# A quarter of the second-table rows of the expert layer moved from TensorE to a sum kept by VectorE

## What is computed

```python
act = gelu(einsum('thkd,td->thk', u_tab[expert], x))       
out = einsum('thk,thkd->td', gate * act, v_tab[expert])    
x = layer_norm(ALPHA * x + out, ln2_g, ln2_b)
```

## Time and profile before

| | |
|---|---|
| median of three runs | 4074.74 us (4070.53 to 4085.25) |
| the profiled execution, own time | 4068.89 us |
| its span | 4067.1 us |
| mean granted TensorE clock | 0.94 |
| TensorE busy | 3526.3 us, 87% |
| VectorE busy | 2538.4 us, 62% |
| ScalarE busy | 1025.4 us, 25% |
| POOL busy | 2533.5 us, 62% |
| moved by DMA | 1270.02 MB, mean 312 GB/s |

### The profile page before, as it was taken

One profiled execution on the slowest core, in us unless ns is written; L12 is line 12 of the kernel. 1 busy time (PEld: TensorE's weight loads), 2 busy tenths in 40 slices (PEclk: granted clock), 3 DMA queues, 4 the chain that ended last, 5 costly groups with the idle time before them and its releaser, 6 DMA issues. The chain is left out here.

```text
span 4067.1 us, 42088 instructions
## 1 busy us (share of the span) xinstructions
PE 3526.3 (87%) x13480; PEld 2019.6 (50%) x13480; DVE 2538.4 (62%) x6604; ACT 1025.4 (25%) x2150; POOL 2533.5 (62%) x2420
## 2 busy tenths in 40 slices
PE   8787698999999799798999799999999877787878
PEld 6576364555555365344566256545555434222434
DVE  2535986766357985667557985567636798645442
ACT  2231132332122223222322222233312222211211
POOL 0212447877675655877765655687766666777773
PEclk9778799999999899999999999999999989999999
DMA  5015888888999898888999988888999989999996
GB/s 183 21 64 183 287 328 320 302 322 328 350 356 372 324 354 333 320 312 294 349 340 386 364 289 318 290 320 308 339 336 343 379 301 358 385 374 362 370 398 228
DMA packets 331050, 1270.02 MB, mean 312 GB/s; under 512 B 38336, under 2 KB 39616, under 8 KB 313808
## 3 DMA queue, kind: packets, MB, share of 16 engines
q0 software_dynamic: 299520, 1090.65, 73.0%
q1 hardware_dynamic: 31312, 176.67, 11.4%
HBM read 1259.74 MB, written 7.44 MB: 312 GB/s over the span
## 5 line engine op out<-in xcount | busy, mean ns | idle before, releaser
L819 PE MATMUL Y<-GV,DIAG 128*128 128x512 f32 x4096 | 1993.3, 624 | 315.4 <-DMA GV<-in_vtab,IDX 249.9
L1759 DVE SCALAR_TENSOR_TENSOR GU<-GU,X 128x1024 f32<-128x1024 f32 x1024 | 1241.4, 1230 | 511.2 <-DMA GU<-in_utab,IDX 508.9
L1038 POOL DMA_INDIRECT GU<-in_utab,IDX x1024 | 1152.5, 1125 | 641.4 <-DVE GU L1759 295.8
L1038 POOL DMA_INDIRECT GV<-in_vtab,IDX x1024 | 1146.1, 1119 | 597.8 <-PE Y L819 374.2
L819 PEld LDWEIGHTS Y<-GV,DIAG 128*128 128x128 f32 x4096 | 767.2, 197 | 1285.1 <-issue 985.9
L514 PE MATMUL A<-XT,WR 128*128 128x264 f32 (+1 forms) x2496 | 579.8, 388 | 18.1 <-ACT R L1252 10.5
L1285 ACT ACTIVATE DIAG<-C,WGT 128x128 f32<-128x128 f32 x1024 | 371.5, 392 | 749.1 <-PE Y L819 625.8
L514 PEld LDWEIGHTS A<-XT,WR 128*128 128x128 f32 x2496 | 481.3, 193 | 146.2 <-issue 74.9
L974 POOL TENSOR_TENSOR R<-R 128x256 f32<-128x256 f32 (+3 forms) x256 | 130.1, 541 | 164.6 <-DVE R L1437 88.9
L567 PE MATMUL SCP<-R,C 128*32 128x64 f32 (+3 forms) x512 | 104.6, 361 | 109.9 <-DVE R L1469 109.6
L733 PE MATMUL D<-WR,R 96*128 96x256 f32 (+3 forms) x800 | 189.9, 395 | 11.5 <-POOL R L992 11.5
(11 more groups left out here) (216 smaller groups left out, 2897.3 us busy)
## 6 DMA issues: line engine op xcount, KB each, us to landing
WR<-in_wstream SPq DMA_DIRECT2D x96, 1024.0 KB, 7.8
WR<-in_wstream SPq DMA_DIRECT2D x36, 1280.0 KB, 9.1
GU<-in_utab,IDX POOLq DMA_INDIRECT x1024, 6.5
GV<-in_vtab,IDX POOLq DMA_INDIRECT x1024, 6.5
R<-in_lnp SPq DMA_DIRECT2D x14, 512.0 KB, 7.1
SS<-in_st_in SPq DMA_DIRECT2D x12, 384.0 KB, 4.8
out_st_s<-SS SPq DMA_DIRECT2D x12, 384.0 KB, 6.2
WR<-in_wstream SPq DMA_DIRECT2D x16, 256.0 KB, 6.5
```

Of the source, the lines that this page charges most:

```text
L819: last = nc.tensor.matmul(Y[0:rows, c], scaled, GV[:, v % RV, c], start=(j == 0), stop=(j == end - 1))
L1038: pool.indirect_dma_start(ring[:, i % places, :], None, table, bass.IndirectOffsetOnAxis(ap=idx, axis=0)).then_inc(fetched[i % places], 16)
L1759: nc.vector.scalar_tensor_tensor(out=u, in0=u, scalar=1.0, in1=X[:, tile_of(g), :], op0=ALU.mult, op1=ALU.mult, accum_out=SCORE[:, g % 2, ...
```

## The change

Rows of a block are divided between two engines. `by_vector` names the entries for VectorE: in blocks 0 to 5 slots 6, 10, ..., 126; in the last 24 entries of the kernel every odd slot below 127. For such an entry there is no diagonal and no matmul; VectorE multiplies the row by the tokens' weights and adds it to `YS`, a new tile in SBUF, one tick later than TensorE had it, ahead of the dot. ScalarE starts `YS` as ALPHA times X, one tick after the block's slot 0, and at the block's end VectorE adds `YS` and `Y` into X. The places of `GV` that VectorE empties are refilled on its signal `v_added`, by a fetch that POOL issues one tick later than before and ahead of that tick's first-table fetch. The 4 KB of `YS` come from `SG` and `SCS`, which now lie over `S`.

```diff
+TAIL = NROW - LAG
+def by_vector(v):
+    kind, _, j = ROWS[v]
+    if kind == "s" or not 4 <= j < SLOTS - 1:
+        return False
+    return j % 4 == 2 if v < STEP_AT[3] else v >= TAIL and j % 2 == 1
+VEC = [by_vector(v) for v in range(NROW)]
+VEC_NO = [sum(VEC[:v + 1]) for v in range(NROW)]
+PE_NO = [v + 1 - VEC_NO[v] for v in range(NROW)]
+DIAGONALS = [v for v in range(NROW) if ROWS[v][0] == "b" and not VEC[v]]
...
+        YS = sb("YS", 128, D)
...
-        SG = sb("SG", 128, 2, 256)
+        SG = view(12400, 2, 256)
+        SCS = view(12912, 2, 2 * NKEY)
...
             def accumulate(v):
                 kind, g, j = ROWS[v]
+                if VEC[v]:
+                    return
...
-                    pe.wait_ge(sems["diag_ready"], v + 1 - sum(r[0] == "s" for r in ROWS[:v]))
-                    scaled, rows, end = DIAG[:, v % NDIAG, :], 128, SLOTS
+                    pe.wait_ge(sems["diag_ready"], DIAG_NO[v] + 1)
+                    scaled, rows, end = DIAG[:, DIAG_NO[v] % NDIAG, :], 128, SLOTS
...
+            def late(i):
+                return i >= RV and VEC[i - RV]
             def fetch_v(i):
-                if i >= RV:
-                    pool.wait_ge(sems["v_used"], i - RV + 1)
+                if i >= RV and VEC[i - RV]:
+                    pool.wait_ge(sems["v_added"], VEC_NO[i - RV])
+                elif i >= RV:
+                    pool.wait_ge(sems["v_used"], PE_NO[i - RV])
                 fetch(GV, vtab, v_fetched, RV, i)
...
+                if 0 <= t - 1 + RV - LAG < NROW and late(t - 1 + RV - LAG):
+                    fetch_v(t - 1 + RV - LAG)
                 if 0 <= t + RU < NROW:
                     fetch_u(t + RU)
-                if 0 <= t + RV - LAG < NROW:
+                if 0 <= t + RV - LAG < NROW and not late(t + RV - LAG):
                     fetch_v(t + RV - LAG)
...
+            def begin_sum(t):
+                if t < LAG + 1 or t - LAG - 1 >= NROW:
+                    return
+                v = t - LAG - 1
+                kind, g, j = ROWS[v]
+                if kind == "b" and j == 0 and g in SHARED:
+                    if v:
+                        act.wait_ge(sems["y_read"], groups_before(v))
+                    nc.scalar.activation(YS[:, :], X[:, tile_of(g), :], ACT.Copy, scale=ALPHA) \
+                        .then_inc(sems["sum_begun"], 1)
...
+            def add_row(v):
+                _, g, j = ROWS[v]
+                dve.wait_ge(sems["sum_begun"], SHARED.index(g) + 1)
+                dve.wait_ge(v_fetched[v % RV], 16 * (v // RV + 1))
+                dve.drain()
+                nc.vector.scalar_tensor_tensor(out=YS[:, :], in0=GV[:, v % RV, :], scalar=WGT[:, g % 2, j:j + 1],
+                                               in1=YS[:, :], op0=ALU.mult, op1=ALU.add).then_inc(sems["v_added"], 1)
...
-                dve.wait_ge(sems["v_used"], v + 1)
+                dve.wait_ge(sems["v_used"], PE_NO[v])
+                if kind == "b" and g in SHARED:
+                    dve.drain()
+                    nc.vector.tensor_tensor(x, YS[:, :], Y[:, :], ALU.add).then_inc(sems["y_read"], 1)
+                    return
...
             for t in range(NTICK):
+                if t > LAG and VEC[t - LAG - 1]:
+                    add_row(t - LAG - 1)
                 if t < NROW:
                     dot(t)
```

More of the change, by code:

```diff
@@ L80, with groups_before @@
 NTICK = NROW + LAG
+TAIL = NROW - LAG
[8 more added lines that the diff above has]
+DIAGONALS = [v for v in range(NROW) if ROWS[v][0] == "b" and not VEC[v]]
+DIAG_NO = {v: k for k, v in enumerate(DIAGONALS)}
+SHARED = sorted({ROWS[v][1] for v in range(NROW) if VEC[v]})
+def groups_before(v):
+    return len({r[:2] for r in ROWS[:v]})
 def tile_of(g):
@@ L281 @@
 rms_ready on_scaled on_ready mv_ready rstd_ready x1_ready x2_ready sg_used lb_ready small_init
-u_used v_used idx_ready top_read gate_ready gelu_ready w_ready diag_ready y_read
+u_used v_used v_added sum_begun idx_ready top_read gate_ready gelu_ready w_ready diag_ready y_read
 sample_found sample_gate sample_known sample_idx sample_gelu sample_w""".split()
@@ L367, in build @@
         WGT = sb("WGT", 128, 2, SLOTS)
-        SCS = sb("SCS", 128, 2, 2 * NKEY)
         EFS = sb("EFS", 128, 2, TOPK)
@@ L804, in accumulate @@
                 kind, g, j = ROWS[v]
[L805 to L808, removed]
+                if VEC[v]:
+                    return
+                if j == 0 and v:
+                    pe.wait_ge(sems["y_read"], groups_before(v))
                 if kind == "b":
-                    pe.wait_ge(sems["diag_ready"], v + 1 - sum(r[0] == "s" for r in ROWS[:v]))
-                    scaled, rows, end = DIAG[:, v % NDIAG, :], 128, SLOTS
+                    pe.wait_ge(sems["diag_ready"], DIAG_NO[v] + 1)
+                    scaled, rows, end = DIAG[:, DIAG_NO[v] % NDIAG, :], 128, SLOTS
                 else:
@@ L1278, in diagonal @@
                 kind, g, j = ROWS[v]
-                if kind == "s":
+                if v not in DIAG_NO:
                     return
@@ L1282, in diagonal @@
                     act.wait_ge(sems["w_ready"], PH * g + j // TOPK + 1)
-                if v >= NDIAG:
-                    act.wait_ge(sems["v_used"], v - NDIAG + 1)
-                nc.scalar.activation(DIAG[:, v % NDIAG, :], ident, ACT.Copy, scale=WGT[:, g % 2, j:j + 1]) \
+                k = DIAG_NO[v]
+                if k >= NDIAG:
+                    act.wait_ge(sems["v_used"], PE_NO[DIAGONALS[k - NDIAG]])
+                nc.scalar.activation(DIAG[:, k % NDIAG, :], ident, ACT.Copy, scale=WGT[:, g % 2, j:j + 1]) \
                     .then_inc(sems["diag_ready"], 1)
+            def begin_sum(t):
[8 more added lines that the diff above has]
+                        .then_inc(sems["sum_begun"], 1)
             def exps(t):
@@ L1328, in _ @@
                     diagonal(t + AHEAD - LAG)
+                begin_sum(t)
                 work.run(t)
```

## The result

The changed kernel takes 4055.2 us in the median, the kernel before, measured beside it, 4073.4. The ratio is 0.9937 with a 95% interval of 0.9919 to 0.9955: faster by 0.6%. The medians lie 18 us apart, the ratio is worth 26 us, and the two profiled executions, 4068.89 and 4052.73 us, lie 16 us apart; forecast were 63, to 4006 us. One of the six executions took 4140.8 us at a granted clock of 0.844; it counts in the median and not in the ratio. The span of the profiled one is 4050.9 us.

What follows compares the result with a forecast made beforehand. No one engine bounds every stage; POOL's in-order fetch queue paces ticks, its waits on TensorE limiting the gain. Closings 27, middles 35, openings 0, block ends -8, tail 9: 63 us off 4068.9, so 4006 us, range 3905 to 4090.

Steps and rivals of the forecast that it cites:

- Closings: Closing stages: 48 rows relieve TensorE of 83 us, but DMA has little room; gain 27 us (0 to 35).
- Middles: the failed step: Middle stages: two thirds of POOL's 90 us waits on TensorE gained, 25 us charged for VectorE; net gain 35 us.
- Openings: the second mis-sized term: Opening stages: half of relief and add cost shows, plus 40 and minus 31, stretched fetches 9; net 0.
- The clock, a term put at nothing: TensorE's granted clock: at about 80% busy it need not fall, so no term was given.
- Tail and block ends: Last 24 rows split between both engines, gain 9 us; VectorE's add of row 126 at six block ends, minus 8 us.
- VectorE holds POOL off: Rival: each of 138 adds in openings and middles costs its full 1.3 us; 51 us slower, 4120 us; chance 0.12.
- the 0.38 us that I charged for each add: Openings and middles: fetches stretched by VectorE's adds, 2 times 0.19 us per pass, half of it let show.
- Nothing comes through: Rival: middles even because POOL's queue is the bound, closings give 16 us, tail and block ends cancel; 4052 us, chance 0.15.
- the signs named in advance: Closings: TensorE under 90%, DMA share 0.97 or more; POOL waits some 150/at most 320 us; openings unchanged; mean fetch under 1.2 us.

Runs made afterwards that it cites:

- e1: Changed kernel without VectorE's 197 adds; TensorE stays relieved of those rows, which are left out of the output: 3982.5 us, 0.9761 of the kernel before.
- e13: Kernel before with 91 rows taken from TensorE in the middles only, still fetched but added by nobody: 4044.4 us, ratio 0.9925.
- e7: Kernel before with three rows of four (270) left out in the middles only, without an add: 4009.6 us, ratio 0.9838.
- e2: TensorE adds all rows as in the kernel before, and VectorE makes the 197 adds too, into an unread sum: 4125.0 us, ratio 1.0123.
- e5: Changed kernel with VectorE taking its rows only in the openings, none in middles, closings or tail: 4105.2 us, 1.0068 of the kernel before.
- e8: e1 with four matmuls of zeros on TensorE ahead of 36 waits for the score products: 3971.6 us, 0.9744 of the kernel before.
- e9: e6 with four matmuls of zeros on TensorE ahead of 36 waits for the score products: 4011.9 us, 0.9840 of the kernel before.
- e14: e13 with those 91 rows not fetched either: 3993.0 us, 0.9799 of the kernel before.
- e15: e1 with a POOL memset of 512 columns in each of the 384 ticks of the middles: 4070.8 us, 0.9994 of the kernel before.
- e6: Changed kernel with VectorE taking its rows in middles, closings and tail, none in the openings: 4019.5 us, 0.9859 of the kernel before.

## Why the prediction was wrong

The direction and the mechanism of the closings were right; the size was off by a factor of more than two, because two terms of the sum were too large. By stage the forecast was 27 + 35 + 0 - 8 + 9 = 63 us; the profiled execution gives 26 in the closings, 5 in the middles, -22 in the openings, 6 in the tail and 2 in the last loop.

**Closings: right.** Forecast 27 us shorter, measured 26. Expected was a DMA share of 0.97 or more: 0.99, 0.99, 0.96. TensorE stayed at 93, 93 and 92%, not under 90. The transfers ran at 385, 382 and 362 GB/s in the closings. The Trainium skill (SBUF — State Buffer, A bandwidth-pool intuition that's wrong) gives some 358 GB/s between HBM and a core; the trace does not agree: two of the three closings are some 7% above it, so it was rightly not used as the limit.

**Middles: the failed step.** I bounded the gain by POOL's 90 us of waits on TensorE and took two thirds, 60. The bound held; the share was mis-sized. The relief alone brought 20 (e1) and 25 (e13). POOL's waits on TensorE in the three middles of e1:

```profile
POOL GV L1065 <- PE Y L846: 13.2, 14, 4.5
...
POOL GV L1065 <- PE Y L846: 18.3, 19, 3.0
...
POOL GV L1065 <- PE Y L846: 27.3, 17, 3.7
```

Of the 90 us, 59 are still there, though a quarter of the rows no longer wait for TensorE; only when three rows of four were gone (e7) did 70 of them go. POOL comes sooner to a row that does wait, and finds it less far on, since its own queue fills most of the stage; that is my reading, and no run shows it by itself. The prediction put that queue at 89% by a gap of 0.30 us ahead of each of 768 fetches. POOL's waits in the three stretches count 646 such gaps (put down to issue), 187 us in all, so it is 1225 of 1418 us, 86%. I used it only for a rival, not for the term. What the term left out altogether are POOL's waits for VectorE's dots in the same stretches, 102 us and more than those on TensorE:

```profile
POOL GU L1038 <- DVE GU L1759: 29.2, 10, 7.0
...
POOL GU L1038 <- DVE GU L1759: 29.7, 13, 4.7
...
POOL GU L1038 <- DVE GU L1759: 42.7, 13, 6.4
```

In e1 77 us of them are still there (22.3, 20.5, 33.7). Against the gain I charged 25 us for VectorE; the adds alone cost 9 (e2), and the changed kernel lies some 15 us above e1. Net forecast a gain of 35, measured 5.

**Openings: the second mis-sized term.** The cost was right in size: forecast 31 + 9 = 40 us, measured 42 (e2) and, against e1, 42. That its second part, fetches stretched by the adds, is not what e2 shows (below) makes the close agreement in part luck. The relief was put at half of 81 us, 40, because TensorE and VectorE were both 83 to 84% busy; e1 gives 20. VectorE, in whose order the search, the dots and the adds stand, paces the openings more than TensorE, so equal busy shares do not mean an equal claim. POOL's waits in the four openings of the kernel before say so: 158 us for VectorE's dots, 99 us for TensorE. The first opening:

```profile
POOL GU L1038 <- DVE GU L1759: 85.3, 36, 8.3
POOL GV L1038 <- PE Y L819: 20.0, 14, 2.9
```

In the changed kernel those on VectorE, dots and adds together, are 227 us and those on TensorE 43. No run changed VectorE's order there, so the pacing is read from these waits with e1 and e2, not tested. Net forecast 0, measured +22, and e5 shows the loss by itself.

**The clock, a term put at nothing.** The prediction took the last loop, 0.96 with TensorE 78% busy, as a sign that the relief would not lower the clock. It did: to 0.87, 0.87 and 0.92 in the middles with TensorE 83, 81 and 87% busy. What that costs is open, some 10 us or nothing by e8 and e9.

**Tail and block ends.** Tail forecast -9, measured -6; from the last dot the last row was done after 38.5 us, where the prediction said about 34, and the sum came after 38.6 us for 44.6. The charge of 8 us for the block ends is not seen in TensorE's waits for the sum into X, before and after:

```profile
PE Y L819 <- DVE X L1805: 33.8, 7, 8.8
...
PE Y L846 <- DVE X L1865: 28.2, 5, 9.9
```

**The rivals.** VectorE holds POOL off: an average fetch took 1.15 us for 1.12, far from the 1.3 us that would have shown it. The adds did not even do that. The first two lines are e1, which has no add, the last two e2, which has all of them:

```profile
L1065 POOL DMA_INDIRECT GU<-in_utab,IDX x1024 | 1179.8, 1152 | 618.4 <-DVE GU L1808 272.1
L1065 POOL DMA_INDIRECT GV<-in_vtab,IDX x1024 | 1160.7, 1133 | 512.5 <-issue 246.5
...
L1063 POOL DMA_INDIRECT GV<-in_vtab,IDX x1024 | 1149.1, 1122 | 660.2 <-PE Y L844 285.2
L1063 POOL DMA_INDIRECT GU<-in_utab,IDX x1024 | 1156.6, 1129 | 623.7 <-DVE GU L1806 271.0
```

Against the 2299 us that the 2048 fetches took before, e1 has 42 us more and e2 7. So the 0.38 us that I charged for each add is not there (7 us are 0.04 an add), and why the fetches of e1 are longer no run shows; the adds cost 51 us in all (e2), 0.26 us each, in some other way. What e2 does show is POOL waiting for the adds themselves, 136 us behind `YS`, while its waits on TensorE's rows fall from 374 to 285. By the Trainium skill (SBUF — State Buffer, SBUF: two separate sides) a VectorE instruction with two SBUF inputs and a GpSimd one that reads SBUF lock each other out for the whole instruction. These traces show at most single fetches held in this way, such as the one of 7.21 us; the mean does not show it. "Nothing comes through" at 4052 came nearest, and its reason for the middles, POOL's queue, is what e14 and e15 support. That its total fits is luck: it gave the closings 16 us, where 26 came, and had no loss in the openings, where 22 went.

Of the signs named in advance, POOL's waits on TensorE fell as said (147 for "some 150"), and the mean fetch stayed under 1.2 us. Those on VectorE rose to 233 + 114 = 347 us, over the 320 that I had allowed: the 114 are the ring's places that now come free only when VectorE is there. TensorE in the closings and the length of the openings missed too.

## What to carry to other kernels

Moving work from the busiest engine to a less busy one pays in the stages where that engine ends the waits and the other has room, so decide it by stage: here 61 rows in closings and tail gain 51 us, and 45 more in the openings cost 29. A queue that feeds every engine in order, such as POOL's fetches, has to be counted with its gaps; here it filled 86% of the middles, and a relief of TensorE by 157 us gave 20. The waits on the relieved engine bound the gain, but a quarter of the rows gone ended only a third of them. Before pricing a relief by the waits that it ends, ask what share of the stage the next queue already fills, and what else that queue waits for.

## What was not expected

- The version that gives VectorE no row in the openings (e6) runs in 4019.5 us, and with zeros ahead of the score waits (e9) in 4011.9; their spreads overlap (4010.6 to 4022.4 us and 4006.2 to 4018.0 us), and the middles, where the zeros stand, grew by 8. Both are faster than the changed kernel (4055.2).
- TensorE's mean granted clock fell from 0.94 to 0.904 with a fifth less row work (197 of 1024 rows), and to 0.75 to 0.80 in e7's middles. Its row matmuls averaged 660 ns for 624, and its busy time fell by 232 us where 197 rows of 1.73 us would make 341. That this lengthened the kernel is neither shown nor excluded: e8 and e9, with more clock, lie 11 and 8 us under e1 and e6, within the spread of these runs.
- Two short memsets on POOL cost nothing, since they fit into the 0.30 us that pass ahead of a fetch.
